# PEER mixer: the first 128 instead of 96 prompt tokens go through gathered expert rows, and activations and gates get another layout in DRAM

## The reference

```python
def one_block(xb):
    q = (xb @ w_q).reshape(PEER_BLOCK, PEER_HEADS, 2, PEER_HALF)
    s1 = jnp.einsum('thd,kd->thk', q[:, :, 0], sub_k1)      # 128 keys each
    s2 = jnp.einsum('thd,kd->thk', q[:, :, 1], sub_k2)
    v1, i1 = lax.top_k(s1, 16)
    v2, i2 = lax.top_k(s2, 16)
    cand = v1[..., :, None] + v2[..., None, :]              # 256 pairs
    top_s, top_pos = lax.top_k(cand, 16)
    eidx = ...                                              # i1 * 128 + i2 of the chosen pairs
    gate = jax.nn.softmax(top_s, axis=-1)
    act = jax.nn.gelu(jnp.einsum('thkd,td->thk', expert_u[eidx], xb))
    return jnp.einsum('thk,thkd->td', gate * act, expert_v[eidx])
```

## Time and profile before

| | us |
|---|---|
| median of 3 runs (lowest, highest) | 3715.84 (3708.44, 3722.89) |
| profiled execution, its span | 3715.8 |
| key phase s, layer 0 and 1 | 740.7 and 735.8 |
| value phase y, layer 0 and 1 | 598.9 and 596.2 |
| TensorE busy, VectorE busy | 3517.8 and 2481.2 |

### The profile page before, as it was taken

How to read it: one execution, slowest core, us unless ns; L and a number is a source line. 1 busy time by engine, 2 the same in 40 slices (tenths; PEclk the granted TensorE clock), 3 DMA queues, 4 the chain that set the end, 5 groups by cost and what they waited for, 6 DMA issues and landing times.

```text
span 3715.8 us, 61775 instructions
## 1 busy us (share of the span) xinstructions
PE 3517.8 (95%) x21277; PEld 3348.0 (90%) x21277; DVE 2481.2 (67%) x5400; ACT 1361.9 (37%) x1938; POOL 1842.5 (50%) x1172
## 2 busy tenths in 40 slices
PE   7999999999999999999888689999999999999998
PEld 7999999999999999999773359999999999999998
DVE  3342597777775777775678543679697876777774
ACT  3322343534444333333221353344435353333332
POOL 3434456555655555552541234456565655555551
PEclk9999999999999999999998699999999999999999
DMA  3222367877788999994346322467777879999982
GB/s 131 80 69 91 103 188 247 277 247 262 262 281 274 298 310 313 324 320 154 99 116 179 105 74 91 136 193 249 268 240 277 274 282 277 297 326 311 329 295 97
DMA packets 392484, 812.36 MB, mean 219 GB/s; under 512 B 52104, under 2 KB 249672, under 8 KB 384888
## 3 DMA queue, kind: packets, MB, share of 16 engines
q1 hardware_dynamic: 171600, 458.35, 37.0%
q0 software_dynamic: 64608, 230.73, 18.1%
q10 hardware_dynamic: 156048, 120.37, 11.0%
HBM read 695.39 MB, written 112.74 MB: 217 GB/s over the span
## 4 chain that ended last, share of the span: by engine, by line
PE 66%; DVE 16%; DMA 7%; issue 4%; ACT 2%; POOL 2%; SPq 2%; another core or an unknown queue 0%; ACTq 0%; DVEq 0%; POOLq 0%
PE acc L638 42%; PE acc L625 15%; DMA rows<-u_in,expertP 4%; PE misc L774 3%; DVE rows L1838 3%; DMA raw<-slabs_in 2%; POOL w_lo L2274 1%; DVE misc L1773 1%; DVE route L1777 1%; DVE hot_gate L1876 1%; PE misc L814 1%; ACT w_hi L1104 1%; DVE work L1716 1%; DVE keyi L1724 1%; PE misc L843 1%
## 5 line engine op out<-in xcount | busy, mean ns | idle before, releaser
L2274 POOL TENSOR_TENSOR w_lo<-raw,w_hi 128x1024 fp32r<-128x1024 f32 x365 | 892.6, 2446 | 1079.8 <-ACT w_hi L1104 1078.6
L638 PE MATMUL acc<-h_hi,w_hi 128*128 128x416 f32 x3072 | 1097.7, 357 | 0.2 <-POOL h_lo L2316 0.2
L638 PE MATMUL acc<-h_lo,w_hi 128*128 128x416 f32 x3072 | 1085.9, 353 | 0.0
L638 PE MATMUL acc<-h_hi,w_lo 128*128 128x416 f32 x3072 | 1081.2, 352 | 0.0
L1104 ACT ACTIVATE w_hi<-raw 128x1024 fp32r<-128x1024 f32 x617 | 653.3, 1060 | 1090.0 <-DMA raw<-slabs_in 1045.4
L638 PEld LDWEIGHTS acc<-h_hi,w_hi 128*128 128x128 f32 x3072 | 581.2, 189 | 8.5 <-POOL h_lo L2316 0.6
L638 PEld LDWEIGHTS acc<-h_hi,w_lo 128*128 128x128 f32 x3072 | 581.9, 189 | 7.4
L638 PEld LDWEIGHTS acc<-h_lo,w_hi 128*128 128x128 f32 x3072 | 581.3, 189 | 3.9
L1955 DVE TENSOR_TENSOR w_lo<-raw,w_hi 128x1024 fp32r<-128x1024 f32 x252 | 325.4, 1291 | 206.1 <-ACT w_hi L1104 205.5
L1838 DVE CUSTOM_DVE_ANT_0 rows<-acc,rows 128x1024 f32<-128x1024 f32 (+1 forms) x224 | 273.4, 1221 | 205.9 <-DMA rows<-u_in,expertP 183.7
L638 PE MATMUL acc<-y_hi,w_hi 128*128 128x416 f32 x1024 | 362.1, 354 | 10.3 <-DVE y_lo L1947 4.3
(11 more groups left out here) (349 smaller groups left out, 5549.4 us busy)
## 6 DMA issues: line engine op xcount, KB each, us to landing
raw<-slabs_in SPq DMA_DIRECT2D x617, 512.0 KB
act_d<-gelu SPq DMA_DIRECT2D x256, 208.0 KB
gate_d<-gout SPq DMA_DIRECT2D x52, 1024.0 KB
abuf<-act_d ACTq DMA_DIRECT2D x32, 1664.0 KB
gbuf<-gate_d ACTq DMA_DIRECT2D x30, 1664.0 KB
unit<-ck_in SPq DMA_DIRECT2D x72, 128.0 KB
vquad<-cv_in SPq DMA_DIRECT2D x64, 128.0 KB
unit<-ck_in ACTq DMA_DIRECT2D x56, 128.0 KB
```

Of the source, the lines that this page charges most:

```text
L638: last = pe.matmul(acc[:, 0, par, 0:ND], w[:, c, :], m(c), start=c == 0 and w is w_hi[r] and m is m_hi, stop=c == KC - 1 and w is w_lo[r])
L2274: pool.tensor_tensor(w_lo[r][:], raw[r][:], w_hi[r][:].bitcast(F32), ALU.subtract).then_inc(lo_done, 1)
```

## The change

`ND` becomes 384, so `D0` is 128: all of block 0 is sparse, and the dense part is exactly blocks 1 to 3. Every dense matmul has 384 columns. There are 9 sparse groups and 144 dots and values in a layer. `STEPS_OF` becomes (0, 16, 16, 16): block 0 has no gate steps and no transposed route, and 12 slabs without gates stand at the end. The dots are spread anew (16 in the window of block 0, 12 in the others, 24 in each block's gate steps, 20 at the end), and the values go eleven to nine slabs. Transposes of group rows stand elsewhere, and group sums of the y phase stand behind slabs by `GROUP_END`.

`act_d` becomes [32, P, 4, ND] and `gate_d` [16, P, 24, 8, 16]: a partition's share of a group of 8 slabs is read in two runs of 6,144 bytes and in one of 12,288. A store of 16 tokens' gates now writes 16 runs of 512 bytes per partition.

ScalarE's gelu of the dots moves behind the last slabs of s, and VectorE prepares the first group of y before it waits for that gelu.

```diff
 TG = 16
-ND = 416
+ND = 384
...
         log_bank = [acc[:, 0, 0], acc[:, 0, 1], misc[:, 3]]
-        act_d = [nc.dram_tensor(f"act_d{l}", [NK, P, ND], F32).ap() for l in range(2)]
-        gate_d = [nc.dram_tensor(f"gate_d{l}", [NG, P, NK, TG], F32).ap() for l in range(2)]
+        act_d = [nc.dram_tensor(f"act_d{l}", [NK // 4, P, 4, ND], F32).ap() for l in range(2)]
+        gate_d = [nc.dram_tensor(f"gate_d{l}", [NK // GRP, P, NG, GRP, TG], F32).ap() for l in range(2)]
...
         OPS = 2 * NDOT
-        WINDOW_DOTS = 12
-        STEP_DOTS = [[1] * 4, [1] * 4 + [0, 0] + [2, 1, 2, 1, 2, 2, 1, 2, 1, 2]]
-        at_slab = []
+        WINDOW_DOTS = [16, 12, 12, 12]
+        STEP_DOTS = [[], [1] * 4 + [2] * 8 + [1] * 4, [1] * 8 + [2] * 8, [1, 2] * 8]
+        at_slab, op_slab = [], 0
             lead = 5 if b == 0 else 3
-            at_slab += [SLAB0[b] + lead + i * (ROUTE_SLABS[b] - lead - 1) // WINDOW_DOTS for i in range(WINDOW_DOTS)]
-            for r, n in enumerate(STEP_DOTS[b > 0]):
+            n_dots = WINDOW_DOTS[b]
+            at_slab += [SLAB0[b] + lead + i * (ROUTE_SLABS[b] - lead - 1) // n_dots for i in range(n_dots)]
+            for r, n in enumerate(STEP_DOTS[b]):
                 at_slab += [SLAB0[b] + ROUTE_SLABS[b] + r] * n
-        at_slab += [NK + i for i in range(NDOT)]
+        TAIL_DOTS = NDOT - len(at_slab)
+        at_slab += [S_DONE + i * (NK - S_DONE - 3) // TAIL_DOTS for i in range(TAIL_DOTS)]
+
+        def values_by(n):
+
+            return min(NDOT, ((n + 1) * 11 + 8) // 9)
+
+        at_slab += [NK + n for n in range(NK) for _ in range(values_by(n) - (values_by(n - 1) if n else 0))]
         assert len(FETCH_AT) == OPS
+        GROUP_END = [next(n for n in range(NK) if values_by(n) >= (g + 1) * TOPK) for g in range(NGR)]
+        assert GROUP_END[-1] + 5 <= NK - 6
...
                     sp.wait_ge(acc_free_act, n + (l * NK + 3))
-                    sp.dma_start(act_d[l][n], gelu[:, r % 2, :]).then_inc(act_stored[r % 2], 16)
+                    sp.dma_start(act_d[l][q][:, r, :], gelu[:, r % 2, :]).then_inc(act_stored[r % 2], 16)
...
                     sp.wait_ge(gate_taken, taken)
-                    sp.dma_start(gate_d[l][chunk], gout[cpar][:]).then_inc(gate_stored[cpar], 16)
+                    sp.dma_start(gate_d[l][:, :, chunk].rearrange("j p g t -> p j (g t)"),
+                                 gout[cpar][:].rearrange("p (j g) t -> p j (g t)", g=GRP)).then_inc(gate_stored[cpar], 16)
...
                                     routeP_loaded, 16)
+                        continue
...
                     last.then_inc(h_rows_done, 1)
-                def steps(b, first, count):
-                    with pe.Fori(first, first + count, 4) as i:
+                def steps(b, first, last):
+                    with pe.Fori(first, last, 4) as i:
                             gates(i + (H0 + STEP0[b] + r), r % 2)
-                    done[0] += count
+                    done[0] += last - first
                     B = l * NDB + b
-                    if b:
+                    G = l * (NDB - 1) + b - 1
+                    if b == 1:
+                        pe.wait_ge(route_done, B)
+                    if b > 1:
                         pe.wait_ge(gate_taken, 2 * (H0 + STEP0[b]) + 2)
-                        pe.wait_ge(slotT_done, B)
+                        pe.wait_ge(slotT_done, G)
...
                         pe.wait_ge(s_sc_taken, l + 1)
-                    s_only(2)
-                    group_h(2 * b - 1 if b else 0)
-                    s_only(ROUTE_SLABS[b] - 2)
+                        s_only(2)
+                        group_h(0)
+                        s_only(ROUTE_SLABS[0] - 2)
+                        continue
+                    if b == 1:
+                        s_only(2)
+                        group_h(1)
+                        s_only(ROUTE_SLABS[b] - 2)
+                    if b == 2:
+                        s_only(ROUTE_SLABS[b])
+                    if b == 3:
+                        s_only(12)
+                        group_h(6)
+                        s_only(ROUTE_SLABS[b] - 12)
                     last.then_inc(routeT_done, 1)
-                    if b:
+                    if b == 1:
                         steps(b, 0, 4)
-                        group_h(2 * b)
-                        steps(b, 4, STEPS_OF[b] - 4)
-                    else:
-                        steps(b, 0, STEPS_OF[b])
+                        group_h(2)
+                        steps(b, 4, 12)
+                        group_h(3)
+                        steps(b, 12, 16)
+                    if b == 2:
+                        group_h(4)
+                        steps(b, 0, 12)
+                        group_h(5)
+                        steps(b, 12, 16)
+                    if b == 3:
+                        steps(b, 0, 8)
+                        group_h(7)
+                        steps(b, 8, 16)
+                s_only(2)
+                group_h(8)
...
                     for c in range(GRP):
+                        n = j * GRP + c
                               free=(acc_free_dve, j * GRP + (DVE_TILES[f"y{l}"] + c + 1)))
+                        if n - 3 in GROUP_END:
+                            group_y(GROUP_END.index(n - 3))
                     y_group(j, j % 2)
-                    if j >= 2 and j % 2 == 0 and j // 2 - 1 < NGR:
-                        group_y(j // 2 - 1)
...
                 def load_acts(j, par):
-                    act.dma_start(abuf[par][:], act_d[l][j * GRP:(j + 1) * GRP].rearrange("i p t -> p i t")).then_inc(
+                    act.dma_start(abuf[par][:].rearrange("p (b i) t -> p b (i t)", b=2),
+                                  act_d[l][2 * j:2 * j + 2].rearrange("b p i t -> p b (i t)")).then_inc(
                 def load_gates(j, par):
-                    act.dma_start(gbuf[par][:], gate_d[l][:, :, j * GRP:(j + 1) * GRP, :].rearrange(
-                        "n p i t -> p n i t")).then_inc(group_loaded[par], 16)
+                    act.dma_start(gbuf[par][:], gate_d[l][j]).then_inc(group_loaded[par], 16)
...
                         act.wait_ge(gate_stored[par], (l * NG // 2 + n1 // 2 + 1) * 16)
-                    act.dma_start(gbuf[0][:, n0:n1], gate_d[l][n0:n1, :, 0:GRP, :].rearrange("n p i t -> p n i t")).then_inc(
-                        first_loaded, 16)
+                    act.dma_start(gbuf[0][:, n0:n1], gate_d[l][0, :, n0:n1]).then_inc(first_loaded, 16)
...
                             act.wait_ge(act_stored[par], (l * NK // 2 + 2 * GRP // 2 + 1) * 16)
-                        act.dma_start(abuf[0][:], act_d[l][0:GRP].rearrange("i p t -> p i t")).then_inc(first_loaded, 16)
+                        act.dma_start(abuf[0][:].rearrange("p (b i) t -> p b (i t)", b=2),
+                                      act_d[l][0:2].rearrange("b p i t -> p b (i t)")).then_inc(first_loaded, 16)
-
-                    act.wait_ge(routeT_done, B + 1)
+                    if b == 0:
+                        continue
+
+                    act.wait_ge(routeT_done, l * (NDB - 1) + b)
...
                     done[0] += STEPS_OF[b]
-                act.wait_ge(rows_used, l * OPS + NDOT)
-                act.activation(dots[0:SR, 0], dots[0:SR, 0], ACT.Gelu_apprx_tanh).then_inc(dot_act_done, 1)
-                act.activation(dots[:, 1:NGR], dots[:, 1:NGR], ACT.Gelu_apprx_tanh).then_inc(dot_act_done, 1)
...
                             hi_part(0, c, 0)
+                act.wait_ge(rows_used, l * OPS + NDOT)
+                act.activation(dots[0:SR, 0], dots[0:SR, 0], ACT.Gelu_apprx_tanh).then_inc(dot_act_done, 1)
+                act.activation(dots[:, 1:NGR], dots[:, 1:NGR], ACT.Gelu_apprx_tanh).then_inc(dot_act_done, 1)
...
                                 square(2, i)
-                        if n % TOPK == 1 and 0 < n // TOPK <= NGR:
-                            group_out(n // TOPK - 1)
+                        if n - 1 in GROUP_END:
+                            group_out(GROUP_END.index(n - 1))
...
                 dve.tensor_copy(count_row, iota[:]).then_inc(dve_step, step.up())
-                if B:
-
-                    dve.wait_ge(routeT_done, B)
+                if l * (NDB - 1) + max(b - 1, 0):
+
+                    dve.wait_ge(routeT_done, l * (NDB - 1) + max(b - 1, 0))
...
                     B = l * NDB + b
-                    last_dot = done[0] + WINDOW_DOTS
+                    last_dot = done[0] + WINDOW_DOTS[b]
...
                         shares(SR, 1, routeS, gsumS).then_inc(dve_step, step.up())
-                    dve.wait_ge(slotT_done, B + 1)
+                        continue
+                    dve.wait_ge(slotT_done, l * (NDB - 1) + b)
                     for r in range(STEPS_OF[b]):
-                        for _ in range(STEP_DOTS[b > 0][r]):
+                        for _ in range(STEP_DOTS[b][r]):
                         one_hots(half, max(b * P, D0) - D0 + r * HG, r % 2, half < 2)
```

(18 more changed lines are left out.)

## The result

The changed kernel takes 3800.35 us (median of 4 runs, 3793.09 to 3804.73), the kernel before 3716.28 (4 runs): a ratio of 1.023, 95% interval 1.0206 to 1.0254. It is 2.3% slower; 3632 was predicted. The profiled execution spans 3801.1 us, 85 more than before.

A forecast was written before the change was run, and what follows sets the result against it. TensorE was taken to bound the y phase, and VectorE's routing and the gather chain much of s. Saving 35 us in y and 7 in s, over two layers, gave 84 us less: 3632 us, range 3555 to 3700.

The forecast's parts named there:

- Columns: Dense slabs: 32 fewer columns cut 24 matmuls from 4.545 to 4.205 us, 0.341 less a slab.
- y, the term that failed: Value phase: TensorE work plus present stalls 558.7 us, plus 5 for late slabs: 564, 35 less a layer.
- for slabs that land late: Value phase: 5 us a layer charged because the slack of three slabs shrinks by 1.0 us.
- Gates' reads in runs of 512 B vanish: Value phase: about 25 MB of gates a layer in long runs save some 32 us of DMA time.
- VectorE in y: Value phase: VectorE's work becomes 3.67 us of each 4.205 us slab, so it fits.
- up to the gate steps of block 1: Start of the s phase: gate steps of block 1 begin at 623.5 instead of 644.6, saving 21 us.
- windows of blocks 2 and 3: Routing windows in s: 83.7 and 83.0 us now, still set by VectorE; 4 us saved.
- the three blocks of steps: 48 gate steps in s: 7.1 us with two dots, 6.05 otherwise; 324 against 325.5 now, ends 293 and 355.
- the tail: End of s: 12 slabs instead of 8 and 20 dots, 58 us against 38.5, ends 54 and 75.
- 512-byte stores: Gate stores in s: 512 B runs add 32 us of DMA time a layer, raising the share from 0.77 towards 0.92.
- Rival 4: Value phase: DMA engines carry no more than 318 GB/s, y 641 us, total 3786 us; chance 0.05.
- Rival 2: Value phase: memory holds it at 358 GB/s, y 576 us, s as forecast, total 3656 us; chance 0.14.

The follow-up runs named there:

- e2: The changed kernel with the old layouts of act_d and gate_d, so the token split alone: 3696.22 us, ratio 0.9965 to the kernel before; repeated at 0.9969.
- e13: The changed kernel with only the activations loaded in runs of 1.5 KB, the gates' 12 KB runs kept: 3776.17 us, ratio 1.0193 to the kernel before.
- e6: The changed kernel with the old layouts and value operations on 256 of 1024 columns, other sums left out: 3630.79 us, ratio 0.9887 to the kernel before.
- e10: The changed kernel with the old layouts and value gathers of 128 half rows, halving their bytes: 3686.35 us, ratio 0.9933 to the kernel before.
- e9: The changed kernel with the old layouts and dots over 256 of 1024 columns, other sums left out: 3606.89 us, ratio 0.9722 to the kernel before.
- e3: The changed kernel, gates still stored by group but loaded in 512-byte runs, activations in 1.5 KB runs: 3697.1 us, ratio 0.9968 to the kernel before.
- e7: The changed kernel with the old layouts and value gathers fetching 64 of 128 rows: 3705.11 us, ratio 1.0088 to the kernel before.
- e12: The changed kernel with the same layout, each group load issued as eight DMAs with 3 KB runs: 3722.17 us, ratio 1.0026 to the kernel before.

## Why the prediction was wrong

**Columns.** Right. A dense slab takes 4.21 us where the chain is on TensorE; I had 4.205.

**y, the term that failed.** I had 564 a layer: 5.2 us of old stalls and 5 "for slabs that land late". Measured 630.1, 66 more. The step that failed is "Gates' reads in runs of 512 B vanish", carried on as a pure gain of DMA time. The saving per MB came. What I left out is that the engines take one run from each queue in turn, so that beside runs of 12 KB a slab needs 6.2 us where TensorE uses one up in 4.205. The slabs take 9 to 13 us to land, and three slabs of lead are no longer 13.6 us but 12.6. Phase lengths put the layout at 47 to 53 us a layer (after against e2), of which the 12 KB runs are 40 or more (e13 against e2). By the same measure my 564 is about 559 (before, 598.9 from the end of s is 594 from the first addition), so e2's 573 to 579 leave some 16 us more. I read them as the work of two margins that I held apart, VectorE (0.83) and the DMA engines (0.97, 343 GB/s), each spoiling the other's recovery; e6 and e10 fit that, but it is argued, not shown.

The waits also cost clock, for which the prediction has no term. TensorE's granted clock in y is 0.98 where it was 1.00: behind some of its waits TensorE works for 3 to 7 us at the lower of its two levels (1.2 GHz). By the clock records that is at most 10 us of layer 0 and 17 of layer 1.

**VectorE in y.** I had 3.67 us of work a slab; the windows give 292.73 / 73 = 4.01 in the changed kernel, 300.31 / 80 = 3.75 in e2. The values take 1.28 us as assumed. The difference is the weight split: mean 1.55 us in the changed kernel against 1.24 before, 1.36 in e2. It is no constant: beside GpSimd's subtraction it stretches to 2.5 us in some cases, and what decides that stays open.

**s.** I had 734; it is 754.0. Part by part: up to the gate steps of block 1 192 us (188.9 forecast); windows of blocks 2 and 3 157.4 (162.7); the three blocks of steps 334 (324); the tail 70.1 (58). So the windows were right within 5 us, and the two terms that I had bounded widest went to the upper half (the upper end of the steps, 355, should have read 360 by its own terms). Of the steps, e9 shows that the dots on VectorE set much of the length; I had priced the dots' added row at each step but not the waits that they bring TensorE: 22.3 us for one-hots (7.3), 22.0 for GpSimd's splits and 20.2 for the route (12.7; I had said 12 to 15 us in block 1 alone, and the longest is 7.9). Here too the clock goes with the waits: 0.96 in s of layer 0, 0.99 before, by its records at most 17 of the 20 us by which s missed the forecast. The end of the tail, VectorE in the changed kernel:

```profile
1172.85 1.23 DVE L1878 CUSTOM_DVE_ANT_0 rows<-acc,rows 128x1024 f32<-128x1024 f32 x1 [1.13 <-DMA rows<-u_in,expertP]
...
1174.00 8.19 DVE L1983 TENSOR_TENSOR abuf<-abuf,gbuf 128x384 f32<-128x384 f32 x8
1182.11 6.48 DVE L1990 TENSOR_TENSOR y_lo<-abuf,y_hi 128x384 fp32r<-128x384 f32 x8
```

Twenty dots reach to 1174, and 14.7 us of work for the first y slabs stand behind them. I took this for the cause, but the lengths say otherwise: the last gelu is at 1185.4, so slabs are late too, the DMA share is 0.89, the clock 0.92, and e9 with short dots has the same tail. Gathers and slabs in one stage are what I would look at; no run here takes them apart.

**512-byte stores.** I charged them 32 us of DMA time and kept them as a threat to s. The profile has the packets of the SyncE queue up from 171600 to 264784. The DMA time is there: from 434.6 to 1185 us this queue holds 50.0% of the engines for 117.66 MB, in e2 46.9% for 118.13, 23 us more. A 512 B packet of a store takes 27 ns and one of 8 KB 310, 3.3 us a MB against 2.4. What did not come is a delay: e2 and e3 have the same ratio, and s in e13, which has these stores, is 739/742, shorter than in e2. So the price was nearly right and the threat was not. The Trainium skill's rule (DMA: Bandwidth & Descriptors, "Specifications", full line rate at runs of 512 B and more) gives the outcome, no time lost, but not the packets' times.

**The rivals.** None foresaw this. Rival 4 had the right sign and nearly the right time (3786), by luck: its mechanism, engines stuck at 318 GB/s, is refuted, since they reach 343 in e2 and 350 in e6 over 360 us, 451 in 2 us of the changed kernel. Rival 2, a memory limit with y at 576, describes the split alone well (571 by this measure, 573 to 579 measured, mean 343). The Trainium skill's ceiling (the same page, "Where 436 GB/s comes from", about 358 GB/s) stands above every mean over 1290 to 1650 us, the highest being 350 (e6); the 2-us stretches of 413 and 451 lie above it. It fits as a bound on the mean, but y in e10 fell only to 566 at 279 GB/s, so it does not set y alone.

## What to carry to other kernels

When several queues share the DMA engines, the length of a contiguous run is also the length of a turn. Before lengthening the runs of a bulk load, ask which transfer with a deadline shares the engines, and work out how long its turns then take: here 8 turns a slab against 4.205 us. Here runs of 12 KB beside 4 KB slab packets cost 40 us and more a layer, the 6 KB runs of the activations 1 to 8, and the cheaper bytes bought nothing.
VectorE with 3.67 of 4.205 us a slab and DMA engines at 0.91 (both my forecast) were not two separate margins: e2 missed the forecast of y by some 16 us. Count the stalls that each may cause the other, or forecast the upper half of both.
A saving on TensorE is worth what the next engine leaves of it: in s the dots' width on VectorE, not TensorE's columns, moved the time.

## What was not expected of the hardware

- Cheaper per byte and yet later: group loads at 2.5 us a MB (3.36 before), DMA share down to 0.86 from 0.94, and slab loads of 10.64 us.
- Halving a gather's rows (64 of 128 partitions) made the whole y phase 25 to 30 us longer, and slab packets went from 155 to 179 ns (e7).
- Of two colliding subtractions either can be the one that is stretched, and the distance of their starts does not say which: GpSimd's and VectorE's took 1.68 and 1.23 us with starts 0.49 us apart, 1.03 and 2.52 with 0.40; behind a wait of VectorE none of 20 of its splits was slow, without one 16 of 23.
- An engine takes one run from each queue in turn, whatever its length: 42, 42 and 44 packets of three queues in 2 us beside 12 KB runs, 93, 94 and 91 beside 512 B runs.
- Eight DMA issues in a row took ScalarE 5.5 us (e12).
- Two chips gave the kernel before 3673 and 3709 us, with mean granted clocks of 0.983 and 0.978.
